# First block's experts: every expert's weights loaded once through three slots, split per block, three-pass products

## What is computed

```python
for e in range(N_EXPERTS):                      # 16
    hid = jax.nn.silu(h @ w_gate[e]) * (h @ w_up[e])      # 1024 -> 256
    y = y + gates[..., e:e + 1] * (hid @ w_down[e])       # 256 -> 1024
```

## Time and profile before

| | us |
|---|---|
| median of the runs (4837.59 to 4840.08) | 4838.89 |
| the profiled execution's own time | 4844.55 |
| its span | 4842.7 |
| `experts_one`, from the last step of `place_tokens` to the first work of `combine_norm` | 402 |

### The profile page before, as it was taken

One profiled execution on the slowest core, in us unless ns is written; L12 is line 12 of the kernel. 1 busy time (PEld: TensorE's weight loads), 2 busy tenths in 40 slices (PEclk: granted clock), 3 DMA queues, 4 the chain that ended last, 5 costly groups with the idle time before them and its releaser, 6 DMA issues. The chain is left out here.

```text
span 4842.7 us, 51793 instructions
## 1 busy us (share of the span) xinstructions
PE 3779.2 (78%) x17638; PEld 2726.6 (56%) x17638; DVE 2579.2 (53%) x4297; ACT 1820.0 (38%) x2807; POOL 341.6 (7%) x280
## 2 busy tenths in 40 slices
PE   7972598789927877896749999688778967499995
PEld 3431266644416755475637777577544756377774
DVE  1896353511142156354188888621554541888886
ACT  1101253022222135333136667521453331377774
POOL 0001100000030000100001111001001000011110
PEclk9985699899968989898769999899899987699998
DMA  2000002089961110001239999711100012499997
GB/s 109 18 0 15 0 1 80 36 312 337 336 232 57 37 25 1 18 1 70 105 125 350 355 358 359 256 53 36 25 9 10 1 70 105 145 360 362 364 358 253
DMA packets 274948, 695.37 MB, mean 144 GB/s; under 512 B 16336, under 2 KB 24912, under 8 KB 272720
## 3 DMA queue, kind: packets, MB, share of 16 engines
q1 hardware_dynamic: 258784, 634.85, 36.2%
q0 software_dynamic: 15984, 58.20, 4.2%
HBM read 630.60 MB, written 62.39 MB: 143 GB/s over the span
## 5 line engine op out<-in xcount | busy, mean ns | idle before, releaser
L2199 DVE TENSOR_TENSOR low_ring<-mix,high_ring 128x2048 fp32r<-128x2048 f32 x384 | 869.1, 2287 | 168.0 <-ACT high_ring L2148 167.3
L2148 ACT ACTIVATE high_ring<-mix 128x2048 fp32r<-128x2048 f32 x384 | 732.2, 1924 | 455.1 <-DMA mix<-in_w_up 174.0
L2089 PE MATMUL ps<-high_ring,x_high 128*128 128x512 f32 x1024 | 414.4, 405 | 55.7 <-DVE low_ring L2199 42.9
L2090 PE MATMUL ps<-low_ring,x_high 128*128 128x512 f32 x1024 | 402.2, 393 | 0.0
L2091 PE MATMUL ps<-high_ring,x_low 128*128 128x512 f32 x1024 | 401.8, 392 | 0.0
L2089 PEld LDWEIGHTS ps<-high_ring,x_high 128*128 128x128 f32 x1024 | 193.4, 189 | 131.8 <-DVE low_ring L2199 68.5
L436 ACT ACTIVATE probs<-logits,less 128x384 f32<-128x384 f32 (+7 forms) x224 | 155.8, 695 | 237.2 <-DVE less L477 237.1
L406 PE MATMUL ps<-ident,probs 128*128 128x128 f32 x1608 | 233.0, 276 | 3.7 <-ACT probs L436 3.5
L1593 PE MATMUL ps<-w_up_ring,xs 128*128 128x512 f32 x496 | 219.7, 596 | 0.7 <-ACT xs L1629 0.7
L2091 PEld LDWEIGHTS ps<-high_ring,x_low 128*128 128x128 f32 x1024 | 193.5, 189 | 42.0
L2090 PEld LDWEIGHTS ps<-low_ring,x_high 128*128 128x128 f32 x1024 | 193.8, 189 | 37.0
(11 more groups left out here) (401 smaller groups left out, 7105.4 us busy)
## 6 DMA issues: line engine op xcount, KB each, us to landing
mix<-in_w_gate SPq DMA_DIRECT2D x128, 1024.0 KB, 6.3
mix<-in_w_up SPq DMA_DIRECT2D x128, 1024.0 KB, 6.3
mix<-in_w_down SPq DMA_DIRECT2D x128, 1024.0 KB, 9.5
w_up_ring<-in_w_gate_up SPq DMA_DIRECT2D x124, 512.0 KB, 5.7
w_down_ring<-in_w_down SPq DMA_DIRECT2D x62, 512.0 KB, 5.1
expert_out<-out SPq DMA_DIRECT2D x31, 512.0 KB, 4.9
w_mix<-in_w_out SPq DMA_DIRECT2D x12, 1024.0 KB, 6.1
w_unit<-in_w_turned SPq DMA_DIRECT2D x10, 1024.0 KB, 4.9
```

Source lines behind the costliest of these rows:

```text
L2089: nc.tensor.matmul(ps[:, bank, :], left_high, high, start=first, stop=False)
L2090: nc.tensor.matmul(ps[:, bank, :], left_high, low, start=False, stop=False)
L2148: nc.scalar.activation(w_high[:, n % RING, :], raw[:, n % RAW_UNITS, :], ACT.Copy).then_inc(high_ready, 1)
L2199: nc.vector.tensor_tensor(w_low[:, n % RING, :], raw[:, n % RAW_UNITS, :], w_high[:, n % RING, :].bitcast(F32), ALU.subtract).then_inc(low ...
```

## The change

What it does:

- The host lays each expert's weights out as one row of 24 KB per partition (`expert_units_1`). SBUF gets three slots of one expert each (`raw_experts`). The first three experts are loaded at the start of `route_one`, by SyncE. In `experts_one` SyncE goes through experts 3 to 15 once, in order, one transfer of 3 MB each, when the splits of the last block of the expert three before are done.
- `place_tokens` works out two more tables: which slot a block reads (`block_slot`) and where each expert's blocks end (`expert_ends`).
- Per block, ScalarE makes the high parts of five pieces of 128x1024 and VectorE the low parts; the sixth piece has both on GpSimd. The turned rows and the turned hidden rows are split in the same way. Every product of the block is three fp32r matmuls. The splits run two blocks ahead of the down product; the up pieces have one buffer each, the down pieces two.
- The output is copied by ScalarE and VectorE, half each, into two buffers, and stored by ScalarE's queue.
- The layer norm's gain and shift get their own buffers at each use, so that the slots find room.

The core of the diff:

```diff
 # route_one
+        @block.sync
+        def _(sp):
+            for e in range(RAW_SLOTS):
+                sp.dma_start(raw[:, e, :], A["expert_units_1"][e]).then_inc(A["raw_in"][e], 16)
 # place_tokens
-            chain.step(ts(block_expert[:, :], expert[:, :], float(E - 1), None, ALU.min))
+            chain.step(ts(expert[:, :], expert[:, :], float(E - 1), None, ALU.min))
+            nc.vector.tensor_copy(block_expert[:, :], expert[:, :])
+            nc.vector.tensor_copy(expert_ends[:, :], ends[:, :])
+            chain.step(ts(turns[:, :], expert[:, :], float(RAW_SLOTS), None, ALU.is_ge))
+            for n in range(2, (E - 1) // RAW_SLOTS + 1):
+                chain.step(nc.vector.scalar_tensor_tensor(out=turns[:, :], in0=expert[:, :], ...))
+            chain.step(nc.vector.scalar_tensor_tensor(out=expert[:, :], in0=turns[:, :], ...))
+            nc.vector.tensor_copy(block_slot[:, :], expert[:, :])
 # experts_one, SyncE
+                for e in range(EXPERTS):
+                    if e >= RAW_SLOTS:
+                        end = sp.value_load(expert_ends[0:1, e - RAW_SLOTS:e - RAW_SLOTS + 1], ...)
+                        sp.wait_ge(down0_low_ready, end + 1)
+                        sp.wait_ge(down1_low_ready, end + 1)
+                        sp.dma_start(raw[:, e % RAW_SLOTS, :], A["expert_units_1"][e])...
+                    if e >= 1:
+                        sp.wait_ge(raw_in[(e - 1) % RAW_SLOTS], 16 * ((e - 1) // RAW_SLOTS + 1))
+                        sp.sem_inc(raw_ready, 1)
 # GpSimd
+                def gather(s):
+                    pool.wait_ge(x_turned, 2 * s)
...
+                def low_down(s, half):
+                    slot = slot_of(pool, s)
+                    pool.wait_ge(down0_high_ready, s + 1)
+                    pool.wait_ge(down_used, 2 * s - 2)
+                    nc.gpsimd.tensor_copy(down_high[:, one, :], down_raw(slot, 1))...
+                    nc.gpsimd.tensor_tensor(down_low[:, one, :], down_raw(slot, 1), down_high[...], ALU.subtract)...
+                def step(b, half):
+                    gather(b + 3)
+                    low_down(b + 2, half)
 # TensorE
+                def product(bank, left_high, left_low, right_high, right_low, first, final):
+                    nc.tensor.matmul(ps[:, bank, :], left_high, right_high, start=first, stop=False)
+                    nc.tensor.matmul(ps[:, bank, :], left_high, right_low, start=False, stop=False)
+                    return nc.tensor.matmul(ps[:, bank, :], left_low, right_high, start=False, stop=final)
+                def step(b, half):
+                    turn_rows(b + 2)
+                    up(b + 1, 1 - half, (0, 1))
+                    turn_hid(b)
+                    up(b + 1, 1 - half, (2, 3))
+                    down(b, half)
 # ScalarE
+                def step(b, half):
+                    slot = begin(s)        # s = b + 2: two value loads, wait for raw_ready
+                    high_x(s, half)
+                    high_up(s, slot, 0)
+                    store(b - 1, 1 - half)
+                    high_hid(b)
+                    high_up(s, slot, 1)
+                    high_up(s, slot, 2)
+                    gate(b + 1, 1 - half)
+                    high_up(s, slot, 3)
+                    high_down(s, slot, half)
+                    keep(b, half)
 # VectorE
+                def step(b, half):
+                    low_x(s, half)
+                    low_up(s, slot, 0)
+                    low_hid(b)
+                    low_up(s, slot, 1)
+                    low_up(s, slot, 2)
+                    hidden(b + 1, 1 - half)
+                    low_up(s, slot, 3)
+                    low_down(s, slot, half)
+                    keep(b, half)
```

More of the change, by code:

```diff
@@ L1313, in _, with route_one @@
             nc.vector.tensor_tensor(logit, made, bias[:, :].unsqueeze(1).broadcast_to([P, T, W]), ALU.add)
-def route_one(book, logit, picked, weights):
+def route_one(book, A, logit, picked, weights, raw):
     nc = book.nc
@@ L1532, in _ @@
             @block.sync
             def _(sp):
[L1534 to L1546, removed]
@@ L1566, in gather @@
                     pool.wait_ge(ready, 1)
-                    pool.wait_ge(ready, 1 if isinstance(b, int) else b)
+                    pool.wait_ge(ready, 1 if isinstance(s, int) and s == 0 else s)
                     pool.indirect_dma_start(taken[:, :], None, A["normed"],
@@ L1605, in down @@
-                    pe.wait_ge(hid_read, b + 1)
-                    for n in range(DOWN):
-                        pe.wait_ge(unit_in[UP + n], 16 * b + 16)
-                        for h in range(2):
-                            last = nc.tensor.matmul(ps[:, 4 + h, :], hidt[:, n, :], w_down[:, n, tile(h, HALF)],
-                                                    start=(n == 0), stop=(n == DOWN - 1))
-                        last.then_inc(unit_used, 1)
+                def down(b, half):
+                    pe.wait_ge(h_low_ready, b + 1)
+                    if not isinstance(b, int) or b >= 1:
+                        pe.wait_ge(out_by_act, b)
+                        pe.wait_ge(out_by_dve, b)
+                    for j in range(2):
+                        if j == 0:
+                            pe.wait_ge(down0_low_ready, b + 2)
+                        else:
+                            pe.wait_ge(down1_low_ready, b + 2)
+                        for h in range(2):
+                            last = product(5 + h, h_high[:, tile(j)], h_low[:, tile(j)],
+                                           down_high[:, 2 * half + j, tile(h, HALF)],
+                                           down_low[:, 2 * half + j, tile(h, HALF)], j == 0, j == 1)
+                        last.then_inc(down_used, 1)
@@ L1621, in _, with high_x @@
-                up(BLOCKS - 1)
-                down(BLOCKS - 1, True)
+                up(0, 0, (0, 1, 2, 3))
+                steps(pe, step)
             @block.scalar
             def _(act):
-                def copy_x(b):
+                def high_x(s, half):
+                    if not isinstance(s, int) or s >= 2:
+                        act.wait_ge(up_used, 4 * s - 4)
                     for h in range(2):
-                        act.wait_ge(x_turned, 2 * b + h + 1)
-                        nc.scalar.activation(xs[:, 4 * h:4 * h + 4, :].rearrange("p a b -> p (a b)"), ps[:, 2 + h, :],
-                                             ACT.Copy).then_inc(x_read, 1)
@@ L1662, in combine_norm @@
+                nc.vector.memset(silu[:, 0:1], 0.0).then_inc(down0_low_ready, 1)
+                for s in range(2):
+                    slot = slot_of(dve, s)
+                    low_x(s, s)
+                    for n in range(4):
+                        low_up(s, slot, n)
+                    low_down(s, slot, s)
+                hidden(0, 0)
+                steps(dve, step)
 def combine_norm(book, A, slots, weights, rows, gain, shift, stats, after):
```

281 lines of the change are left out of this document (200 added, 81 removed).

## The result

| | us |
|---|---|
| median of the changed kernel (4863.62 to 4872.11) | 4867.9 |
| median of the kernel before, beside it (4836.29 to 4840.08) | 4838.89 |
| ratio, with its 95% interval | 1.0059 [1.0044, 1.0074] |
| span of the profiled execution | 4870.0 |

4800.5 was predicted, with a range from 4772 to 4843. The change made the kernel slower by 0.6%, and the prediction was wrong in sign and in size.

What follows compares the result with a forecast made beforehand. TensorE bounds the kernel before, DMA 4% behind; afterwards VectorE and the gather's loop, 10.6 us a block. Stage -53.7, tables +13.7, placing +1.6 make -38.4: from 4838.9 to 4800.5 us, range 4772 to 4843.

Steps and rivals of the forecast that it cites:

- TensorE's part: Experts' stage, per block: three-pass products 8.1 us, turning rows 1.04, hidden rows about 0.3, together 9.44.
- Ahead of the stage: Before the experts' stage: small tables land behind three expert loads, +13.7 us, and placing's extra steps, +1.6.
- Rival 1: Before the experts' stage: the small tables don't wait behind the weights, so 4787 us in all; chance 0.12.
- The gather's loop: Experts' stage: the gather stands behind low_down on GpSimd's queue and TensorE needs its rows; 21.3 us for two blocks.
- rival 2: Experts' stage: TensorE is the bound, gathers land in 4.4 us, a block takes 9.5, 4770 in all; chance 0.12.
- The clock: TensorE in the experts' stage: granted clock stays full at 1.00; under 0.95 would void TensorE's sum.
- VectorE's 10.6: Experts' stage, per block: VectorE's own work 9.35 us plus 1.2 of waiting for GpSimd on the SBUF port.
- ScalarE: Experts' stage, per block: ScalarE's work sums to 9.7 us, from 7.7 to 11.3, near TensorE and below VectorE.
- DMA's part: Experts' stage: 73.5 MB move in under 220 us at 335 GB/s, can't bind on the mean; costed at nothing.
- Fill: Start of the experts' stage: gather(2) lands 28 us in, TensorE then begins step 0, down(0) ends about 36 in.
- Rival 3: Experts' stage: GpSimd holds the loop, 12.2 us a block, 4850 in all; chance 0.17 from 11.6 a block up.
- Rival 4: Experts' stage: loads bind or the loop isn't as written, 11 to 11.5 us a block, 4812 to 4826; chance 0.09.

Runs made afterwards that it cites:

- both_narrow: Kernel `both` with GpSimd's copy and subtraction of the sixth piece cut to 8 columns, output not the reference's: 4754.5 us, ratio 0.9825.
- two_taken: Changed kernel with two buffers for the gathered rows, and the gather of block b+4 issued ahead of low_down(b+2): 4781.5 us, ratio 0.9869.
- both: Changed kernel with two buffers for the gathered rows and the small tables loaded ahead of the first three expert loads: 4771.1 us, ratio 0.9841.
- tables_first: Changed kernel with the first three expert loads issued behind the four small tables, in place_tokens: 4855.3 us, ratio 1.0040.
- no_late_loads: Changed kernel without the 13 transfers of experts 3 to 15 in the experts' stage, output not the reference's: 4810.6 us, ratio 0.9944.
- paced_loads: Changed kernel with each late expert load in six transfers of 512 KB, at most two in flight: 4841.0 us, ratio 0.9989.
- low_later: Changed kernel, one buffer for gathered rows, with GpSimd doing low_down(b+1) in step b instead of low_down(b+2): 4818.7 us, ratio 0.9957.

## Why the prediction was wrong, step by step

**TensorE's part: right.** 9.44 was worked out; its own step is 9.33 in `both_narrow`, and `two_taken` and `both` run at 9.41.

**Ahead of the stage: right.** +15.3 forecast, +15.6 in the trace, with the tables near 962.4 forecast and 962.71 seen. Part of it is confirmed by undoing it (13.65 us less of waiting in the trace of `tables_first`, 9 us of time, give or take 10). Rival 1 falls.

**The gather's loop: right mechanism, wrong size; this is the step that failed.** The term is the gather's landing, taken at 5.5 us and measured at 9.85 beside a load, with what its wait drags along. The prediction's sum for two blocks was 0.1 + 4.3 + 1.0 + 6.4 + 0.1 + 9.4 = 21.3. Behind the last load it is 21.2, and without late loads 21. Beside the loads it is 27.4, and the trace gives each term: from TensorE's last pass to the end of GpSimd's two 4.8 (5.3 forecast with VectorE's wait), the index copy and its wait 1.9 (0.9 forecast), landing 9.85 (5.5), TensorE's step 10.8 (9.4). The sum is 27.4, 6.1 over, of which 4.35 are the landing and 1.4 the step. The forecast took the landing from the kernel before, where a saturated queue still let a gather land in 5.5, and concluded that fewer bytes could only be quicker. It even reckoned with quick gathers in rival 2. It didn't ask what the new load is released by: the end of low_down, with the gather next in the same queue of GpSimd. So in every second block beside the loads the two meet, and the load is all 3 MB at once. `no_late_loads` and `paced_loads` show it.

**The clock.** The prediction let it stand at 1.00, by a stretch with 5% of gaps. After a wait of 7.11 us TensorE's turns take 1.97 us instead of 1.03, the lower of its two levels (1.2 GHz), and the step 10.8 instead of 9.4; after waits of 2.3 us they mostly take 1.09, and the step 9.4. Not always: behind the wait of 2.37 us at 1364.56 in the changed kernel the turns take 1.25, the step 10.96, and the granted clock in it is 0.84; in `no_late_loads` the step after such a wait took 11.0 in 4 of some 14 cases between blocks 3 and 30. The runs don't show what decides it. The stretch beside the loads has 0.87. The prediction named a clock under 0.95 as what would void its sum; it came with the wait, and adds 1.4 us to a pair.

**VectorE's 10.6: wrong, and hidden by the other loop.** From one step's start to the next VectorE takes 9.41 us in `both`, with no gap. Low parts without a port wait step on by 1.13, turned rows by 1.19 for two, the small ones by 0.34, the output by 0.60, sum 8.1; the port waits come to 1.3 (the down piece's low part takes 2.07 instead of 1.22, one up piece's 1.65). I had summed durations, which overlap by 0.06 to 0.09 from one instruction to the next, and 0.4 for a value load of which there is no trace: 9.35. The port term itself (1.2) was right. GpSimd's copy, taken as 1.2 with bounds of 0.945 and 2.35, took 1.04 alone (at the start of `both_narrow`) and 1.6 on the mean in the changed kernel's stage, and its subtraction 2.75. That the two loops seemed to agree at 10.6 made me surer of each, and one of them was off by 1.2.

The rule of the Trainium skill that was named for this ("SBUF — State Buffer", "SBUF: two separate sides") says that the later of the two waits for the whole instruction. Here the trace agrees: 8.66 us for four low parts beside GpSimd's passes, 4.62 without.

**ScalarE: not the bound**, as forecast, but the sum of 9.7 was too high. In `both` it is busy 70.55 of 90 us, 7.4 us a block. The table load is not in the loop (one in the whole stage of the changed kernel, 1.28 us), and the two value loads, taken as 1.0, leave no visible gap.

**DMA's part: right in the mean, wrong as an argument.** 0.56 busy; no wait for raw weights in TensorE's or ScalarE's list. But "it can't bind on the mean" is about bytes, and what bound was how long one small transfer takes behind a large one.

**Fill.** Down(0) was to end 36 us in. It ended 42.4 us in (1030.8): +6.4 of the miss. GpSimd was earlier than forecast (its first pair ended 18.7 us in, not 21.5), but the gather of block 2 landed 11.1 us after its issue, beside the first late load, so TensorE had the rows at 30.8 instead of 28. The step then took 11.65 us. The forecast had left 8 for it, 1.4 less than its own 9.44 for a step: that slip is in the sum itself. The 27 steps that follow make up 27 x (12.77 - 10.6) = 58.6. Together 65 of the 67 us.

**The rivals.** Rival 3 (slower, GpSimd holds the loop) gave the time, 4850, nearest to the measured, and its loop is the right one; but its price came from a slower copy and a slower subtraction with more waiting, 7.4 us together. They took 4.8 in the pair above, less than the 5.3 forecast, and are none of the 6.1. That it came nearest in time is luck. Rival 2 is what `two_taken` turned the kernel into. Rival 4 fell as it was meant: no engine waits for a slot's weights.

What stays open is why a gather behind a deep queue takes 9 us when it is 0.5 MB. The runs say that depth matters and the form doesn't; how the DMA engines divide themselves was not measured. Pacing a load also lowers the rate at which that load runs, and no run takes the two apart; that gathers landed in 5.5 beside a steady 335 GB/s before speaks against the rate.

## What to carry to other kernels

When a change removes traffic, ask not only how many bytes are left but what releases each transfer, how much is asked for at once, and which small transfer on the path is issued right behind it; a landing time read beside a steady stream doesn't hold beside a burst. A prefetch that stands on a queue behind a computing step waits for that step's inputs too: give it a second buffer and issue it first, before anything else is tuned. And add up an engine's period from start-to-start steps, not from durations.

## What the runs showed of the hardware that was not expected

- A 0.5 MB gather landed in 4.7 us (median) without loads beside it, in 6.6 with at most 1 MB queued, and in 8.6 to 9.3 with 3 MB queued on another engine's queue just ahead of it, whether these were one transfer or six, in runs of 2 to 24 KB. The medians are over a stretch in which only some gathers meet a load. In `two_taken`, where the gather is issued at another time, the median was 5.0 beside the same 3 MB transfers, and the longest 15.1.
- The cost of GpSimd's SBUF passes beside VectorE depends on where in VectorE's step they fall: a block took 9.4 us with them at its end (`both`), and 10.4 with them in its middle (`low_later`, behind the last load), at the same work.
- GpSimd's 128x1 index copy, 0.18 us before, took 1.18 where it fell beside a low part of VectorE, and ended within 0.1 us of that low part (1211.72 against 1211.67): a tiny operation waits for the whole of the other's instruction too.
